# The experts' return by norm weights behind the transposes, and no idle transposes on TensorE

## The reference

```python
def first_block(x, ...):                       # 2 layers
    y = mixer(x, ...)                          # three attentions, gates, w_o
    x = layer_norm(DN_ALPHA * x + y, ln1_g[l], ln1_b[l])
    y = moe(x, router_w, router_b, w_gate, w_up, w_down)   # 16 experts in 4 groups, 2 of one group
    x = layer_norm(DN_ALPHA * x + y, ln2_g[l], ln2_b[l])
# second block, 2 layers: rms_norm before and after each of
#   swiglu_ffn (width 2816, halved), hybrid_mixer, swiglu_ffn (halved)
def hybrid_mixer(h, w_in, conv_w, ...):
    proj = h @ w_in
    branches = [stick_breaking_attention(q, k, v),
                silu(layer_norm(depthwise_conv(a * sigmoid(g)))),
                rms_norm(gla_chunked(...)) * silu(r)]
    return sum(sigmoid(gate_i) * (branch_i @ w_branch_i)) @ w_out
```

## Time and profile before

| | |
|---|---|
| three runs | 2379.73, 2383.12 and 2384.64 us; median 2383.12 |
| the profiled execution | 2383.86 us; its span 2382.3 us |
| mean granted TensorE clock | 0.994 of 2.4 GHz |
| busy: PE, DVE, ACT, POOL | 96, 74, 59, 10% of the span |
| PE instructions | 11114 |

### The profile page before, as it was taken

One profiled execution on the slowest core, in us unless ns is written; L12 is line 12 of the kernel. 1 busy time (PEld: TensorE's weight loads), 2 busy tenths in 40 slices (PEclk: granted clock), 3 DMA queues, 4 the chain that ended last, 5 costly groups with the idle time before them and its releaser, 6 DMA issues.

```text
span 2382.3 us, 39448 instructions
## 1 busy us (share of the span) xinstructions
PE 2298.4 (96%) x11114; PEld 1875.9 (79%) x11114; DVE 1755.2 (74%) x2348; ACT 1409.6 (59%) x1892; POOL 236.9 (10%) x296
## 2 busy tenths in 40 slices
PE   9998999999998999999999999999999999989998
PEld 7777788878777788877887867888878877778887
DVE  6778888887778888897556788765565568887555
ACT  5653777774653777774446576454464466765445
POOL 0000000000000000000000692000000008800000
PEclk9999999999999999999999999999999999999999
DMA  7444899985444799995555544565656554455652
GB/s 263 129 144 133 303 340 332 345 326 160 151 135 152 277 336 335 342 333 191 185 185 177 163 140 150 186 205 185 193 188 186 184 179 141 156 170 161 211 184 97
DMA packets 277777, 497.33 MB, mean 209 GB/s; under 512 B 20512, under 2 KB 112848, under 8 KB 277632
## 3 DMA queue, kind: packets, MB, share of 16 engines
q1 hardware_dynamic: 273440, 481.60, 60.6%
q0 software_dynamic: 4192, 14.02, 2.0%
HBM read 494.50 MB, written 1.05 MB: 208 GB/s over the span
## 4 chain that ended last, share of the span: by engine, by line
PE 69%; DVE 14%; DVEq 6%; issue 4%; ACT 3%; DMA 1%; ACTq 1%; PEldq 0%; SPq 0%; PEld 0%; POOLq 0%
PE g_bank L625 14%; PE g_bank L626 13%; PE g_bank L627 13%; PE s_bank L627 8%; PE s_bank L625 8%; PE s_bank L626 8%; DVE w_lo L598 4%; DVE conv_y L2700 2%; DVEq L2694 1%; PE t_bank L1783 1%; DVEq L2304 1%; ACT w_hi L593 1%; PE t_bank L1943 1%; DVE row_max L2328 1%; PE t_bank L1807 0%
## 5 line engine op out<-in xcount | busy, mean ns | idle before, releaser
L598 DVE TENSOR_TENSOR w_lo<-w_raw,w_hi 128x1024 fp32r<-128x1024 f32 x909 | 1095.7, 1235 | 337.0 <-ACT w_hi L593 312.2
L593 ACT ACTIVATE w_hi<-w_raw 128x1024 fp32r<-128x1024 f32 x909 | 944.5, 1058 | 408.1 <-PE g_bank L627 170.3
L625 PE MATMUL g_bank<-w_hi,xt_hi 128*128 128x512 f32 (+1 forms) x1136 | 453.8, 399 | 11.5 <-ACT gate L1401 5.1
L626 PE MATMUL g_bank<-w_lo,xt_hi 128*128 128x512 f32 (+1 forms) x1136 | 442.6, 390 | 0.0
L627 PE MATMUL g_bank<-w_hi,xt_lo 128*128 128x512 f32 (+1 forms) x1136 | 442.4, 389 | 0.0
L625 PEld LDWEIGHTS g_bank<-w_hi,xt_hi 128*128 128x128 f32 x1136 | 215.6, 190 | 67.0 <-issue 13.4
L627 PEld LDWEIGHTS g_bank<-w_hi,xt_lo 128*128 128x128 f32 x1136 | 215.2, 189 | 45.3
L626 PEld LDWEIGHTS g_bank<-w_lo,xt_hi 128*128 128x128 f32 x1136 | 215.6, 190 | 40.3
L625 PE MATMUL s_bank<-w_hi,xt_hi 128*128 128x512 f32 x608 | 240.2, 395 | 0.0
L627 PE MATMUL s_bank<-w_hi,xt_lo 128*128 128x512 f32 x608 | 237.3, 390 | 0.0
L626 PE MATMUL s_bank<-w_lo,xt_hi 128*128 128x512 f32 x608 | 236.9, 390 | 0.0
(11 more groups left out here) (366 smaller groups left out, 2887.2 us busy)
## 6 DMA issues: line engine op xcount, KB each, us to landing
w_raw<-in_w_in_dram SPq DMA_DIRECT2D x192, 512.0 KB, 4.6
w_raw<-in_moe_w_gate_dram SPq DMA_DIRECT2D x128, 512.0 KB, 5.3
w_raw<-in_moe_w_up_dram SPq DMA_DIRECT2D x128, 512.0 KB, 5.6
w_raw<-in_moe_w_down_dram SPq DMA_DIRECT2D x128, 512.0 KB, 5.3
w_raw<-in_ffn_w_gate_dram SPq DMA_DIRECT2D x176, 256.0 KB, 2.9
w_raw<-in_ffn_w_up_dram SPq DMA_DIRECT2D x176, 256.0 KB, 3.1
w_raw<-in_ffn_w_down_dram SPq DMA_DIRECT2D x88, 512.0 KB, 3.4
w_raw<-in_w_branch_dram SPq DMA_DIRECT2D x40, 512.0 KB, 4.4
```

What stands on the lines that cost most here:

```text
L593: nc.scalar.activation(half_of(w_hi, u, h), half_of(w_raw, u, h), ACT.Copy).then_inc(hi_ready, 1)
L598: nc.vector.tensor_tensor(half_of(w_lo, u, h), half_of(w_raw, u, h), half_of(w_hi, u, h).bitcast(F32), ALU.subtract).then_inc(lo_ready, 1)
L625: nc.tensor.matmul(dst, a_hi, b_hi, start=first, stop=False)
L626: nc.tensor.matmul(dst, a_hi, b_lo, start=False, stop=False)
```

## The change

Nothing is computed otherwise but for the order of roundings. Parts that the diff shows or that stand around it:

- **A, return.** PE returns tile 0 whole, then tile 1. DVE takes the statistics of tile 0 between its additions, one half (`held[0]`) is split ahead of the additions where it was four; the others lie between the steps behind. DVE writes only the normalized `acc`; PE turns that. Gain and bias follow behind the transposes, where a channel is a partition: ACT applies them in four activations per quad (`affine`), a fifth rounds; DVE makes `xt_lo` (`affine_lo`). The x in rows that the residual needs is made by POOL (`x_made`), in layer 1 for tile 1 by DVE. POOL loads gain and bias also as columns (4 bytes apart elements), and DVE waits for them ahead of the expert loop. Tile 1's quads come earlier in PE's first products of the next part (`(half, h)`).
- **B.** All idle transposes are gone.
- **C, w_o.** The order of the `out_unit` calls; tile 0's quads come ahead of the last one; in the routing one split of 512 KB less stands ahead of the sigmoid on ACT and of the ranking on DVE, and the fifth half is split inside the gather.
- **D, row_returned.** The second half is scaled behind the first half's sum; a function `between` (xt_lo of tile 1's first quad) stands ahead of the second half's `norm_in`; ACT squares each half as its product ends.
- **G, conv.** Two splits of DVE ahead of `conv_back` where it were four, and ACT loads silu's table behind the convolution's root.

```diff
-    plain()
+    unit()
+    hi()
     step("conv_back", n_t=2)
+    lo()
     plain()
...
                     elif kind == "conv_root":
                         act_root(At(8 + 5, (l, 11)))
+                        act.preload_act_table_set("silu_and_others")
...
+                def affine(tt, kq):
+                    tf = t_next + (2 * tt + kq)
+                    act.wait_ge(t_ready, tf.value(1, 1))
+                    for j in range(4):
+                        k = 4 * kq + j
+                        last = act.activation(xt_full[:, tt, kq, j * P:(j + 1) * P], t_bank[tf.slot(2)][:, j * P:(j + 1) * P], ACT.Identity,
+                                              scale=gain_col[:, 0, k:k + 1], bias=gain_col[:, 1, k:k + 1])
...
+                affine(0, 0)
+                tile_root(1, At(3, (l, 4)))
+                split_hi(u_next, 2)
+                affine(0, 1)
+                split_hi(u_next, 3)
+                affine(1, 0)
+                affine(1, 1)
+                split_hi(u_next, 4)
...
-            def idle_products(bank, n):
...
-                out_unit(0, 1, (0, 1))
+                out_unit(0, 1, (0,))
                 pe.wait_ge(xt_ready, 10 * l + 8)
                 out_unit(1, 0, (0,)).then_inc(wo_ready, 1)
                 out_unit(1, 1, (0,)).then_inc(wo_ready, 1)
+                out_unit(0, 1, (1,))
                 out_unit(1, 0, (1,))
+                x_quads(t + (T_AFTER_MIX1 + 4), 8 * l + 4, 0)
                 out_unit(1, 1, (1,))
...
-                    for groups in (range(NG - 1), (NG - 1,)):
+                    for tt, groups in ((0, range(NG - 1)), (0, (NG - 1,)), (1, range(NG - 1)), (1, (NG - 1,))):
...
+                    pool.dma_start(gain_col[:, i, :], d[w][bass.ds(l, 1), :].rearrange("a (k p) -> p (a k)", p=P), allow_slow_non_contiguous=True).then_inc(gains_in, 16)
...
-                            elif half == 1 and h == 0:
+                            elif (half, h) == ((0, 1) if l else (1, 0)):
...
+                dve.wait_ge(gains_in, 96 * l + 96)
...
+                        if tt == 0:
+                            row_stats(acc, 0, nb)
+                        if i == 1:
+                            variance(0).then_inc(first_var_ready, 1)
...
+                normed(0)
+                for nb in range(2):
+                    row_stats(acc, 1, nb)
+                variance(1).then_inc(var_ready, 1)
+                affine_lo(0, 0)
+                normed(1)
+                split_lo(u_next, 2)
...
+                    dve.drain()
                     dve.wait_ge(square_ready, 15 * l + (sq + 2 * tt + 2))
...
-                    scaled(1)
-                    dve.drain()
                     dve.wait_ge(rstd_ready, At(8 + n + tt, (l, 11)).value(1, 1))
                     for nb in range(2):
+                        if nb:
+                            scaled(1)
+                            dve.drain()
                         dve.scalar_tensor_tensor(out=x[:, tt, cols], in0=dst[:, tt, cols], scalar=rstd[:, tt:tt + 1], in1=x[:, tt, cols],
                                                  op0=ALU.mult, op1=ALU.add)
+                        if nb and between is not None:
+                            between()
```

More of the change, by code:

```diff
@@ L1083, in run @@
                             act.activation(y_hi[:, bass.ds(g, 1), :], s_bank[:, :].unsqueeze(1), ACT.Copy).then_inc(y_hi_ready, 1)
-                    for place in held:
-                        ahead(place)
+                        if what == "gather" and part == "start":
+                            split_hi(at_r["u"], 4)
+                    if held:
+                        split_hi(held[0], AHEAD)
+                for h in range(2, 4):
+                    split_hi(at_r["u"], h)
                 all_parts(act, run)
@@ L1232, in in_root, with square @@
                     act.drain()
[L1234 to L1239, removed]
+                def square(tt, nb, fills, junk, factor):
+                    act.activation(junk[:, nb * 512:(nb + 1) * 512], g_bank[fills[tt][nb].slot(4)][:, :], ACT.Square,
+                                   scale=DM ** -0.5 / factor, accum_out=mean_sq[:, tt, nb:nb + 1])
+                    act.drain().then_inc(square_ready, 1)
                 def root(tt, n):
@@ L2517, in run @@
                                 dve.drain().then_inc(y_ready, 1)
-                        for place in held:
-                            ahead(place)
+                            if what == "gather" and part == "start":
+                                split_lo(at_r["u"], 4)
+                        if held:
+                            split_lo(held[0], AHEAD)
+                    for h in range(2, 4):
+                        split_lo(at_r["u"], h)
                     all_parts(dve, run, make_onehot)
@@ L2532, in _ @@
                 if l < DEPTH - 1:
[L2533 removed]
+                    u_next, n_next, row_sem = layer1(l + 1, done)["u"], At(0, (l + 1, 16)), row_ready
                 elif stacks == 2:
[L2535 to L2547 removed]
@@ new lines, in affine_lo @@
+                def affine_lo(tt, kq):
+                    dve.wait_ge(xt_hi_ready, (n_next + (2 * tt + kq)).value(1, 1))
+                    part = slice(tt * P, (tt + 1) * P)
+                    dve.tensor_tensor(xt_lo[:, 4 * kq:4 * kq + 4, part], xt_full[:, tt, kq, :].rearrange("p (a b) -> p a b", a=4),
+                                      xt_hi[:, 4 * kq:4 * kq + 4, part].bitcast(F32), ALU.subtract)
+                    dve.drain().then_inc(xt_ready, 1)
+                dve.sem_inc(var_ready, 1)
@@ new lines, in _ @@
+                normed(0)
+                for nb in range(2):
+                    row_stats(acc, 1, nb)
[3 more added lines that the diff above has]
+                split_lo(u_next, 2)
+                affine_lo(0, 1)
+                split_lo(u_next, 3)
+                affine_lo(1, 0)
+                affine_lo(1, 1)
+                if l == DEPTH - 1:
+                    for gain_row, op in ((gain, ALU.mult), (bias, ALU.add)):
+                        dve.drain()
+                        for kq in range(2):
+                            cols = slice(kq * 512, (kq + 1) * 512)
+                            dve.tensor_tensor(x[:, 1, cols], (acc if op == ALU.mult else x)[:, 1, cols], gain_row[:, cols], op)
+                    dve.drain().then_inc(x_ready, 1)
@@ L2551, in _ @@
+                split_lo(u_next, 4)
             if stacks < 2:
```

212 lines of the change are left out of this document (121 added, 91 removed).

## The result

The changed kernel takes 2387.36 us (median of 10 runs, 2385.86 to 2389.18), the kernel before in the same rounds 2381.31 us (10 runs). The ratio is 1.0024, its 95% interval 1.0016 to 1.0031: slower by 6.05 us. That is outside the 4.8 us that the prediction called no change, but the interval, 3.8 to 7.4 us, holds 4.8 too. Its profiled execution took 2388.13 us, its span 2386.4, 4.1 us more than the span before. The two traces differ by less than the medians do, because the profiled execution of the kernel before lay 2.5 us above that kernel's median and this one 0.8.

The account below looks back on a forecast made before the run. PE, busy 96% of the time, was taken to bound the kernel through its waits and its clock. Gains and losses summed to 0.5 us slower, 2384.4 on the profiled execution, 2383.7 as median; range 2371 to 2394.

Parts of the forecast that it names:

- B, start: Start: without idle transposes, dense products do the warming at half the clock; 1.9 us lost (0 to 2.2).
- B, routing, both: Routing of both layers: without its 65 transposes the clock falls, slowing gather and first experts' products; 4.4 us lost.
- C, routing, both: Routing, twice: earlier quads of tile 0 and fewer splits ahead of sigmoid and ranking win 2.1 us each, 4.2 together.
- A, layer 0, with its clock: Return of layer 0: first dense matmul earlier, 4.5 us won; new half-clock stretch and slower first transposes, 2.0 lost.
- A, layer 1: Return of layer 1: first dense matmul earlier, 5.8 us won (bounds 4 and 7), no new clock loss.
- G with its clock: Convolution, twice: PE resumes 3.2 us earlier each, 6.4 won; half the clock behind the gate's wait, 3.0 lost.
- D, waits: row_returned, five places: the second gate comes later and PE waits 1.1 us more at each, 5.5 lost.
- D, clock: row_returned: half of the five longer waits cost 1.7 us at half the clock; 4.3 lost (0 to 8.5).
- tail: End of the kernel: DVE's last subtraction and the tail, 0.3 us lost.
- Rival 2: row_returned's second-quad waits cost 14.0 us, not 9.8, and the routing 3.3, not 2.2: 2390 us; chance 0.22.
- Rival 1: Whole kernel: the clock doesn't fall more than now, half or more of 15.6 us stays away: about 2375; chance 0.33.
- Rival 3: Ahead of the expert loop: gain and bias columns land late and DVE waits, 2 x 3 us, 2390; chance 0.08.

Follow-up runs that it names:

- run 11: The changed kernel with only the start's idle transposes back (10 and 24): 2385.72 us, ratio 1.0018 to the kernel before.
- run 12: The changed kernel with only the routings' idle transposes back (20, 11, 16 and 18 in each layer): 2382.44 us, ratio 1.0007 to the kernel before.
- run 4: The kernel before with only the convolution's part of the change: 2376.88 us, ratio 0.9978 to the kernel before.
- run 3: The changed kernel with DVE's row_returned wholly as before, without between and with the second scaling ahead of the root's wait: 2377.84 us.
- run 1: The changed kernel with 234 idle transposes put back at the start, in the routings and in the returns: 2376.92 us.
- run 5: The kernel before with only its idle transposes taken out: 2391.59 us, ratio 1.0040 to the kernel before.
- run 6: The changed kernel with POOL's work for x in layer 0 held back until DVE has made all four xt_lo: 2387.39 us.
- run 7: The changed kernel with tile 1's x rows in layer 1 made by POOL too, not by DVE: 2386.91 us.
- run 8: The changed kernel with the idle transposes back as in run 1 and row_returned as before as in run 3: 2368.04 us.
- run 9: The kernel of run 8 with POOL's work for x held back until xt_lo is made: 2366.42 us.
- run 10: The kernel of run 9 with two weight splits more on ACT and on DVE ahead of the second stack's first root: 2369.00 us.
- run 2: The changed kernel with between gone and the scaling order as changed: 2381.58 us.

## Why the prediction was right or wrong

The forecast was 0.5 us slower (2383.7), the result 6.05 us slower (2387.4, at a kernel before of 2381.3). The time lies in the range (2371 to 2394), even in the likeliest case's own (2379 to 2388), and the sign is the forecast's. But the size is beyond the 4.8 us of "no change", which had the highest chance (0.37; slower had 0.30). The agreement is partly luck: the two returns were forecast at 8.3 us and gave 0.7, and gains elsewhere, some of them not forecast, covered part of that. The terms of the sum, faster being positive, with what traces and runs gave:

| term | forecast | measured | from |
|---|---|---|---|
| B, start | -1.9 | -1.6 | run 11 |
| B, routing, both | -4.4 | -4.9 | run 12 |
| C, routing, both | +4.2 | +4.1 | run 12's trace |
| A, layer 0, with its clock | +2.5 | +0.2 | +3.54 to +3.30 |
| A, layer 1 | +5.8 | +0.5 | +1.97 to +1.50 |
| G with its clock | +3.4 | +4.8 | run 4 |
| D, waits | -5.5 | -6.4 | the table under run 3 |
| D, clock | -4.3 | -3.1 | run 3's 9.5 less the waits |
| expert loops | 0 | +1.9 | +4.15 to +3.54, +3.27 to +1.97 |
| tail | -0.3 | not separated | |
| sum | -0.5 | -4.5 | |

The measured column mixes medians and traces; 1.5 of the 6.05 us stay unplaced, less than the interval of any one run.

- **B, the clock.** Right in mechanism and size. 8.3 us was charged for the start, the routing and layer 0's return; 9.6 was measured for taking all 290 idle transposes out of the kernel before, and 10.4 for putting 234 into the changed one. The gather at 6.65 and 5.26 us lies in the forecast's bounds.
- **The rule that spoke against it.** The Trainium skill ("TensorE: Matmul & The Clock Gate", Part 4: PE-mode transpose) has transposes not count as PE-busy in the way matmuls do, by which the removal would be free. Runs 1, 5 and 12 contradict that here: with float32 transposes of the identity in its gaps the routing had a clock of 1.00, without them 0.68. At the start, where PE had done nothing but transposes, the second dense matmul took 0.40 us before and 0.63 in the changed kernel.
- **D, row_returned.** Right in mechanism, place and nearly in size. The wait was forecast at 2.3 and is 2.29 or 2.30 at all five places; 1.1 us was forecast for each, and PE goes on 1.38 us later at three places and 1.15 at two. The first `gate`, counted 0.4 us earlier, came 0.2 earlier against tile 0's quads at the first place (PE's wait for it fell from 0.49 to 0.28 us). Run 3, without DVE's part of D, won 9.5 us where waits and clock together were forecast at 9.8. "Half of the five cost 1.7" was one of five in the profiled execution. Over the six profiles that have this wait of 2.29 or 2.30 us (the changed kernel and runs 1, 6, 7, 11 and 12) the stretch followed at 10 of 30 places and cost 0.9 to 2.3 us, on average 1.4.
- **G, conv.** 4.8 instead of 3.4. In the changed kernel's first mixer the wait at the gate came out at 1.29 us, not 2.6 (1.87 in the second), and no stretch followed it. PE came later to it there, since it had met a stretch at half the clock behind `conv_y` (1474.74 to 1477.73); the account falls there from +3.89 to +0.35, 3.5 us where 3.2 less 1.5 were forecast. In the second it falls from +4.19 to +2.50, 1.7, just that; there a stretch did follow.
- **A, the returns.** The first dense matmul did come earlier: by 3.6 us in layer 0 (+3.54 to -0.09), 5.3 in layer 1 (+1.97 to -3.36), where 4.5 and 5.8 were forecast. In layer 0 PE idled 2.39 us ahead of the first quad (its row is at 548.95) where 1.7 was counted, and the four activations, rounding and subtraction took 3.94 us where 3.55 was. The step that failed is what the sum assumed behind the first dense matmul: 2.0 us for the clock in layer 0 and nothing in layer 1 ("In layer 1 there is one already"), and 0.3 us for tile 1's quads in each. In layer 0 3.4 us are given back by 575.84's row: 2.5 of slower work, most of it the stretch at half the clock, and 0.85 of waits. In layer 1 4.9 are given back by the hidden rows: 1.9 of slower work (12 dense matmuls of 0.63 us at 1093.94 where it were seven), and 3.0 in the three waits of 0.60, 0.65 and 1.76 us. These are behind ACT's and DVE's programs, which now hold the affine steps, the x rows and the splits of the next unit at once. In layer 0 two losses hide each other: with the clock held PE waits 2.22 us for `xt_lo` instead (run 8), and only with POOL's additions out of DVE's way too is it 3.7 us shorter than before (run 9), near the forecast's 4.5. In layer 1 run 8's profile is 3.2 us shorter than before; there runs 7 and 10 took out some of the waits and left or lengthened the largest, so its cause stays open.
- **C.** Right. In run 12, where the clock is held as before, PE needs 64.33 us from the dense matmul at 174.32 (before; the one released by DVE's `rot`) to the first expert's products in layer 0 and 64.46 in layer 1, where it needed 66.58 and 66.31: 2.25 and 1.85 won. In the changed kernel the lost clock (67.67 and 66.26) hides it.
- **The rivals.** Rival 2, D decides, was nearest in time (2390) but not in cause: D cost about what the forecast had, 9.5 of the rival's 14.0, and what made the kernel slower than forecast is A. Its second part came closer: the gather of layer 0 took 2.8 us more, of its bound 3.3. Rival 1 fell with run 5. Rival 3, late columns, did not occur: no wait of DVE ahead of the expert loop ends on POOL's loads, and the columns landed 4.4 and 5.7 us after their issue.

## What to carry to other kernels

Work that only keeps an engine busy can be worth its place: ask of a removal what the clock does in the gap, and test it both ways, since 290 useless transposes were worth 10 us here. When a chain's steps are reordered to bring one result earlier, price the later one that shares the waiting instruction with it: PE needed both quads, so an earlier first and a later second was a pure loss, five times over. Measure such a loss from a point ahead of both, not by one of the two waits. An earlier start is a gain only if what ran in the time ahead of the old start (splits, squares, side rows) still fits; look at the waits of the next 25 us before booking it. And two causes can cover each other: behind layer 0's return holding the clock alone won nothing (49.83 to 49.61 us), moving POOL's work alone 1.9, and both together 3.7, each read from one profile.

## What the runs showed of the hardware that was not expected

- A wait of 2.29 to 2.30 us was followed by half the clock at one of five places of the changed kernel, and at 10 of 30 in six profiles of nearly the same program, at changing places. Even a wait of 1.49 us was, at the third place of run 2. The price of such a wait is a chance, not a figure.
- POOL's float32 tensor operations beside DVE's lengthened DVE's: a normalizing pass of 128x512 from 0.50 to 0.98 us (half of the rows of two), a subtraction of 128x512 from 0.69 to 1.77, one of 128x1024 from 1.22 to 2.30, and POOL's own pair of 128x512 from 2.49 to 3.79. The Trainium skill ("GPSIMD Engine Reference", 1. Specifications) has the two share SBUF interfaces when a DVE instruction has two SBUF inputs or runs in a two-port mode; the subtractions, with two inputs in SBUF, agree (1.77 against 0.69 us in run 6), and so do DVE's statistics, which have one input and took 1.46 us with POOL beside them and without. In which mode the normalizing pass runs no run here shows.
- At the very start the window's granted clock reads 1.00 in 11.40:16.80, although every dense matmul there takes 0.63 us, the time of half the clock. There only the durations tell it:

```profile
11.40:16.80 5.40, 5.40 (x13) 4.24 (x14) 3.28 (x3) 1.56 (x2) 1.37 (x2) 1.00 1.04 393
```
